# Moving the low-part split of the attention outputs behind the rotation on the vector engine

## The reference

```python
s = jnp.einsum('bnqhgd,bnkhd->bnhgqk', qb, kband) * (SWA_HEAD_DIM ** -0.5)
s = jnp.where(mask[None, :, None, None], s, NEG_INF)
m = jnp.maximum(jnp.max(s, axis=-1, keepdims=True), sink)
p = jnp.exp(s - m)
p = p / (jnp.sum(p, axis=-1, keepdims=True) + jnp.exp(sink - m))
o = jnp.einsum('bnhgqk,bnkhd->bnqhgd', p.astype(v.dtype), vband)
```

## Time and profile before

| | |
|---|---|
| median of 3 runs | 1710.95 us (1707.68 to 1711.09) |
| profiled execution | 1707.68 us, span 1705.7 us |
| granted PE clock, mean | 0.998 |
| busy: PE, weight loads, DVE, ACT, POOL | 98%, 86%, 71%, 43%, 53% |
| window attention, passes u = 2 to 7 | 118 to 188 us of the span |
| DMA | 424.80 MB, 249 GB/s on average |

### The profile page before, as it was taken

How to read it: one execution, slowest core, us unless ns; L and a number is a source line. 1 busy time by engine, 2 the same in 40 slices (tenths; PEclk the granted TensorE clock), 3 DMA queues, 4 the chain that set the end, 5 groups by cost and what they waited for, 6 DMA issues and landing times.

```text
span 1705.7 us, 26673 instructions
## 1 busy us (share of the span) xinstructions
PE 1671.7 (98%) x9077; PEld 1471.7 (86%) x9077; DVE 1209.3 (71%) x2262; ACT 734.3 (43%) x1103; POOL 899.6 (53%) x573
## 2 busy tenths in 40 slices
PE   6999999999999999999999999999999999999998
PEld 6767888888878899999999999999888888888886
DVE  6678521212156699999888888635888888888887
ACT  6478632222242233333466666533333333333334
POOL 7622234444433369998988988885233333333220
PEclk9999999999999999999999999999999999999999
DMA  6211122222322248988889999999999999999992
GB/s 248 99 62 38 50 75 99 99 95 91 109 76 85 87 169 300 322 303 307 300 266 359 329 347 359 341 399 374 411 353 371 378 353 363 380 351 363 377 364 110
DMA packets 127107, 424.80 MB, mean 249 GB/s; under 512 B 13264, under 2 KB 29648, under 8 KB 124880
## 3 DMA queue, kind: packets, MB, share of 16 engines
q1 hardware_dynamic: 80688, 264.28, 42.6%
q0 software_dynamic: 36864, 134.23, 21.2%
q10 hardware_dynamic: 9504, 25.71, 3.8%
HBM read 371.74 MB, written 52.43 MB: 249 GB/s over the span
## 4 chain that ended last, share of the span: by engine, by line
PE 68%; issue 18%; POOL 12%; DMA 1%; ACT 1%; DVE 1%; POOLq 0%; ACTq 0%
PE bank L891 30%; PE bank L523 19%; POOL w_lo L465 11%; PE bank L527 10%; PE both L512 5%; PE bank L879 3%; DMA raw<-stream 1%; PE bank L836 1%; PE bank L791 0%; ACT w_hi L952 0%; POOL rows L486 0%; DVE x_sb L1720 0%; DVE x_sb L1714 0%; ACT junk L1222 0%; POOLq L462 0%
## 5 line engine op out<-in xcount | busy, mean ns | idle before, releaser
L465 POOL TENSOR_TENSOR w_lo<-raw,w_hi 128x1024 fp32r<-128x1024 f32 (+1 forms) x302 | 599.9, 1998 | 398.9 <-ACT w_hi L952 397.6
L952 ACT ACTIVATE w_hi<-raw 128x1024 fp32r<-128x1024 f32 x346 | 367.2, 1061 | 844.7 <-PE bank L891 309.4
L486 POOL DMA_INDIRECT rows<-stream,idx x256 | 295.8, 1155 | 354.4 <-DVE both L1699 299.8
L523 PE MATMUL bank<-hT_hi,w_hi 128*128 128x384 f32 x1024 | 346.8, 339 | 0.5 <-ACT abuf L1159 0.5
L523 PE MATMUL bank<-hT_lo,w_hi 128*128 128x384 f32 x1024 | 342.3, 334 | 0.0
L1684 DVE TENSOR_TENSOR w_lo<-raw,w_hi 128x1024 fp32r<-128x1024 f32 x128 | 156.7, 1225 | 67.6 <-ACT w_hi L952 67.6
L527 PE MATMUL bank<-hT_hi,w_lo 128*128 128x384 f32 x1024 | 198.5, 334 | 1.0 <-POOL w_lo L465 1.0
L891 PE MATMUL bank<-w_hi,wT_hi 128*128 128x512 f32 x768 | 196.0, 389 | 0.7 <-ACT abuf L1159 0.7
L891 PE MATMUL bank<-w_hi,wT_lo 128*128 128x512 f32 x768 | 195.6, 389 | 0.0
L891 PE MATMUL bank<-w_lo,wT_hi 128*128 128x512 f32 x768 | 195.5, 389 | 0.0
L523 PEld LDWEIGHTS bank<-hT_hi,w_hi 128*128 128x128 f32 x1024 | 192.3, 188 | 1.1 <-ACT w_hi L952 0.8
(11 more groups left out here) (285 smaller groups left out, 2409.7 us busy)
## 6 DMA issues: line engine op xcount, KB each, us to landing
raw<-stream SPq DMA_DIRECT2D x346, 512.0 KB, 5.2
a_rows<-abuf ACTq DMA_DIRECT2D x64, 384.0 KB, 5.9
g_rows<-gstage SPq DMA_DIRECT2D x32, 768.0 KB, 8.7
g_in<-g_rows SPq DMA_DIRECT2D x16, 1536.0 KB, 10.3
a_in<-a_rows SPq DMA_DIRECT2D x64, 384.0 KB, 6.6
rows<-stream,idx POOLq DMA_INDIRECT x256, 7.2
x_sb<-x SPq DMA_DIRECT2D x4, 512.0 KB, 8.7
out<-x_sb SPq DMA_DIRECT2D x4, 512.0 KB, 2.6
```

The lines of the kernel that those rows point to most:

```text
L465: last = pool.tensor_tensor(w_lo[:, k % 2, cols], raw[:, k % RAW, cols], w_hi[:, k % 2, cols].bitcast(f32), ALU.subtract)
L486: pool.indirect_dma_start(rows[:, g % SLOTS, :], None, table, bass.IndirectOffsetOnAxis(idx[:, g // HK, g % HK:g % HK + 1], 0)).then_inc(g ...
L523: pe.matmul(dst, w_hi[:, slot, k * P:(k + 1) * P], hT[low][:, k, DENSE], start=(k == 0 and low == 0), stop=False)
L952: act.activation(w_hi[:, base % 2, :], raw[:, slot, :], ACT.Copy).then_inc(hi_ready, 1)
```

## The change

In passes u = 2 to 7 the call of outputs_low moves in DVE's order. Before, it stood between the second and the third group of reductions. Now it stands behind the four groups, negm, sdiff and the rest of the rotation (which pass 7 does not have), and in front of the normalisation. The other engines' programs stay as they are.

```diff
                     if b == 0 and u < 7:
                         rotate_bank(*turned_q)
-                    if b == 1 and u >= 2:
-                        outputs_low(8 + u - 2, 4 + u - 1)
                 dve.wait_ge(score_read, 4 * (u + 1))
                 snk = sinks[:, 2 * u:2 * u + 2].unsqueeze(1).broadcast_to([P, TT, 2])
                 dve.tensor_scalar(negm[:, :], mcap[:, :], -1.0, None, ALU.mult)
...
                 if u < 7:
                     dve.wait_ge(proj_read, R_Q + u + 2)
                     rotate(*turned_q, bank_done=True)
+                if u >= 2:
+                    outputs_low(8 + u - 2, 4 + u - 1)
                 for j in range(2):
                     cols = slice(4 * j, 4 * j + 4)
                     dve.wait_ge(expd, 2 * u + j + 1)
```

## The result

| | before | changed |
|---|---|---|
| median | 1709.58 us (1707.68 to 1711.09, 4 runs) | 1728.47 us (1725.59 to 1733.95, 4 runs) |
| profiled execution | 1707.68 us, span 1705.7 | 1725.54 us, span 1723.5 |
| mean granted PE clock of it | 0.998 | 0.996 |

The ratio is 1.0113, with a 95% interval of 1.0092 to 1.0136: the change makes the kernel slower by 18.9 us. The direction was forecast, the size was not: 1721.6 was predicted, with 1716 to 1726.5 as the range. All 21 runs of the changed kernel on record lie between 1723.71 and 1734.37 us, and the longer ones have the lower mean granted clock: 0.997 in the shortest, 0.989 in the longest.

What follows compares the result with a forecast made beforehand. The tensor engine, busy 98% of the span, was taken as the bound. Slides of 7.6 us plus stalls of 2.6 and 0.5 made 10.7 us, which on the 1710.95 median gave 1721.6 us, range 1716 to 1726.5.

Steps and rivals of the forecast that it cites:

- Where the loss sits: Delay arises in sliding-window attention; from the memory attention on, all times are later by the same 10 to 11 us.
- The wait for y_lo takes the place of the wait for the rotation: On PE, value products wait five times about 2.6 us and once 0.5; the rotation wait nearly goes for u = 3 to 6.
- The 0.61 us by which capped comes earlier: On DVE, capped comes up to 0.61 us earlier; 4 x 0.61 = 2.4 us of PE's query-product waits could be had.
- The size of the stall: PE's first value product comes at R+6.30 instead of R+3.72, a 2.58 us stall; a pass takes 14.00 instead of 12.11.
- In the new order: DVE schedule beside GpSimd's pieces: line 1322 from R+3.76, third piece from R+4.34 holding line 1323, outputs_low issued at R+5.51.
- the sum: Adding up the DVE schedule and stalls: y_lo at R+6.20, stall 2.58 us, in total 7.6 + 2.6 + 0.5 = 10.7 us.
- The lower bound: If none of GpSimd's holding of DVE recurs, y_lo comes at R+5.3, the stall is 1.7, the loss 6.0 us.
- The clock: Whether PE's clock falls behind the attention's stalls: 2.6 us being shorter than a 2.91 us gap, it was expected to stay 1.00.
- by the row nothing happens: Profile row: PE's longest idle in this stretch is 2.91 us, before 107.82; afterwards the granted clock is 1.00, i.e. 2.4 GHz.
- Rival (c): PE's clock falls at each stall, doubling the 5.61 us of work after it in six passes: +34 more, 1755; chance 0.03.
- (a): The y_lo wait on PE has room enough and the shorter vector-scalar loop shows: gain at most 2.4 us, 1708.5; chance 0.06.
- (b): PE's stalls are absorbed where it waited before (3.1 us) and in the stage behind: about 1711 to 1714; chance 0.06.

Runs made afterwards that it cites:

- Experiment 2: Kernel before, outputs_low unmoved; in passes 2 to 6 PE also waits before its first value product until this pass's rotation has ended. 1724.12 us, ratio 1.0094.
- experiment 7: Changed kernel's DVE order, but ACT copies bank 1 to SBUF, outputs_low subtracts from the copy, PE waits for the copy instead of y_lo. 1707.01 us, ratio 0.9987.
- experiment 8: Kernel before with outputs_low directly behind sdiff, and PE doing five of eight query blocks, not four, ahead of the value products. 1706.64 us, ratio 0.9986.
- Experiment 4: Kernel before with outputs_low moved only directly behind sdiff, in front of the rest of the rotation. 1712.42 us, ratio 1.0016.
- experiment 6: Changed kernel with GpSimd's four subtraction pieces of passes 2 to 6 made to wait until outputs_low is through. 1714.78 us, ratio 1.0035.
- experiment 3: Changed kernel with 12 unused matmuls before the y_lo wait in passes 2 to 6 and 12 before pass 1's query product. 1721.39 us, ratio 1.0073.
- experiment 9: Kernel before with 12 matmuls on constant operands filling PE's idle gap in pass 1 only. 1707.93 us, ratio 0.9989.
- experiment 1: Kernel before plus a PE wait before the first value product on the previous pass's rotation, which is always over. 1708.93 us, ratio 1.0.
- experiment 5: Kernel before with only pass 4's outputs_low moved behind the rotation, the other five left in place. 1713.67 us, ratio 1.0027.

## Why the prediction was right in direction and too small

*Where the loss sits.* Right. PE's start of the first memory scores came at 187.34 before and at 205.19 after, 17.85 later, and the whole executions differ by 17.86. Nothing is taken up or lost behind the attention. Timelines of PE, before and changed:

```profile
187.34 1.99 PE L715 MATMUL bank<-kmT,qr 128*128 128x256 f32 x8
```

```profile
205.19 1.99 PE L715 MATMUL bank<-kmT,qr 128*128 128x256 f32 x8
```

*The wait for y_lo takes the place of the wait for the rotation.* Right, with all six places: five long stalls and one of 0.41, the other wait gone from pass 2 on. Experiment 2 makes the loss with the wait alone, experiment 7 removes it by taking the dependence away. The 0.61 us by which capped comes earlier is real too: passes of 11.4 to 11.6 us instead of 12.11 in experiments 7 and 8 fit it.

*The size of the stall.* The term that was mis-sized is the holding by GpSimd's pieces in "In the new order". I had line 1322 start ahead of the third piece, holding it off. In the trace the third piece starts first (about R+3.78, two pieces of 0.70 behind 152.89, against R+3.83 for line 1322), so 1322 waits for it, and 1323 for the fourth: outputs_low ends at R+6.79 where the sum had R+6.20. That makes the stalls 3.04 instead of 2.58 and the passes 14.54 instead of 14.00; the first of them, with no old wait to replace, is 3.10 longer than before, where the sum had 2.58. The two starts were only 0.01 apart in my own schedule (R+3.76 and 3.77), and it was wrong to take one way out of a tie as given. That outputs_low itself isn't held by a piece was right, but the changed kernel does not test it: its pieces have ended (152.89 + 3.25 = 156.14) when outputs_low begins at 156.62. Experiment 4 tests it, with timelines of DVE and POOL: outputs_low lies in the middle of the four pieces and takes 0.68:

```profile
136.08 0.68 DVE L1366 TENSOR_TENSOR yT_lo<-both,yT_hi 128x512 fp32r<-128x512 f32 x1
134.63 3.32 POOL L465 TENSOR_TENSOR w_lo<-raw,w_hi 128x256 fp32r<-128x256 f32 x4 [8.93 <-ACT w_hi L952]
```

The lower bound, y_lo at R+5.3, is what experiment 6 measures (R+5.31), and its median, 6.4 us over before, is near the 6.0 of that bound.

With the second hold, the stalls at full clock come to 3.10 + 4 x 2.43 + 0.48 = 13.3 us instead of 10.7. Experiments 3 and 9, with the gaps filled in both, give 1721.39 - 1707.93 = 13.5 from their medians, or 12.3 + 2.4 = 14.7 if each is taken against the before on its own chip. Put into the forecast, 13.3 would make it 1724.3, still within the range. This term alone does not break it.

*The clock.* This is the step that failed, the term put at nothing: "by the row nothing happens". It rested on a single gap of 2.91 us with the clock up behind it. Behind a gap of the same length in the same place, the clock fell in the changed kernel's profile; that alone is 1.39 us between the two profiled executions (scores of pass 2 at 117.75 against 116.36) and is no effect of the change: in the profile of experiment 1, whose PE and DVE work in the order of before, the first matmul behind this gap also takes 0.76 instead of 0.47, and experiment 9 takes most of the slower runs of before away by filling it. Timeline of PE, experiment 1:

```profile
108.46 0.76 PE L621 MATMUL both<-hT_hi,w_hi 128*128 128x512 f32 x1 [2.90 <-DVE qr L1319]
```

The row was luck. Nine kept profiles have this gap unfilled; the clock fell behind it in seven, all but before's and experiment 6's, and in none of the three where matmuls fill it.

Behind the moved calls the clock fell in two of five stalls of 3.04 us, at 1.6 us each (16.13 - 14.54). 13.3 + 3.2 + 1.4 = 17.9, the difference of the two executions. In the medians what is left for the clock is larger: 18.9 - 13.3 = 5.6 us, as much as three or four falls; the spread of the 21 runs with their mean clocks fits that, though only one of them was traced. A stall of the predicted length would not have kept the clock up either: it fell behind two of the five of 2.57 us in experiment 2.

*Rival (c)* named this mechanism at a chance of 3% and a price of 5.6 us a stall. The mechanism is there, the price is not: PE does not stay at 1.2 GHz for all the work up to the next scores, but is back at 2.4 within the same pass (at 145.91, 4.7 us behind the start at 141.20, before the scores at 148.42). The rule of the Trainium skill that I had weighed (TensorE: Matmul & The Clock Gate, "HAM oscillation — how this bites in real kernels") was the better guide than my one row. It is borne out in part, and by stalls shorter than the waits in the page's own example: stalls that come back in every pass do lower the clock, but not behind each one (two of five here, none behind the 3.08 in experiment 5's profile).

*Rivals (a) and (b)* are refuted: the stall is there in every pass, and experiment 5 shows that even a single one isn't made good. What remains open is which stall the clock falls behind; it differs between executions of one kernel, and short of filling the idle time no run controls it.

## What to carry to other kernels

Before moving an instruction back in its engine's order, list who waits for what it signals, and how much room each has: here a list of waits showed nothing, because the wait was met 1.63 us early, and the move made the signal 4.70 us later. A moved release wants its reader moved too: an order with outputs_low only as far as sdiff gained 1.7 us instead of losing 3.4 once PE did one more block of work in front of its wait (experiments 8 and 4). And price a repeated stall of the tensor engine with and without a fall of its clock: one gap without a fall is no proof.

## What the runs showed of the hardware

- An idle stretch of 2.6 to 3.1 us of PE brings the clock to 1.2 GHz in some executions and not in others, for the same code at the same place (the gap of pass 1: 7 of 9 profiles; stalls of 2.57 us in experiment 2 and of 3.04 in the changed kernel: 2 of 5 each). One fall behind these stalls cost 1.5 to 1.6 us. Behind the gap of pass 1 it cost from 1.6 (changed kernel, 10.11 us from the end of the gap to the scores of pass 2 instead of 8.54) to 2.7 (experiment 1, 11.21). Behind stalls of 0.77 and 1.58 us (experiments 4 and 6) the profiles show none.
- Putting useless matmuls into such gaps made the kernel faster: by 7 us in the changed kernel (six gaps), by 2.4 in the median in the kernel before (one gap; 0.998 to 0.9998 of its time).
- DVE operations with both inputs in SBUF and GpSimd subtractions take turns. The same two rotation steps took 0.69 and 0.69 alone, 0.68 and 1.11 before, 1.22 and 1.10 changed, by the start times depending on which side was first by a few hundredths of a microsecond. negm, an operation with one SBUF input of 8 columns, was held as well (0.69 instead of 0.17). outputs_low, whose first input is in PSUM, was not: 0.68 in the middle of the pieces in experiment 4.
